# Two attention mixers on one core: the next pair's scores move ahead of the odd head's transposes, and four roundings spread over four heads

## What is computed

```python
def layer(x, ctx, ...):
    q, k, v, ga, uf, gf, zc, bc, cc, gc = split_cols(hx @ w_in, PROJ_SIZES)
    q, k = axial_rope(q), axial_rope(k)             # 8 query heads, 2 key heads, 64 wide
    a = window_attention(q, k, v, kc, vc, sink_b)   # softmax with a sink, blocks of 128 queries
    f = fourier_mix(uf, w_fourier)                  # fft2, real part, then a small product
    s = short_conv_mix(zc, bc, cc, conv_w, conv_b)  # three taps
    y = gated_merge(a, ga, f, gf, s, gc, w_out)     # concat(a*silu(ga), f*silu(gf), s*silu(gc)) @ w_out
    x_new = x + gate * rmsnorm(y, g_post)
    # layer 0 does the same for the context tokens (context_attention)

def sink_softmax(s, sink_b):
    m = max(max(s), sink_b)
    e = exp(s - m)
    return e / (sum(e) + exp(sink_b - m))
```

## Time and profile before

| | |
|---|---|
| time, median of 3 runs | 2353.62 us (2348.67 to 2356.35) |
| the profiled execution | 2354.48 us |
| its span | 2352.7 us |
| PE busy | 2259.4 us, 96% of the span |
| DVE / ACT / POOL busy | 1145.2 (49%) / 857.0 (36%) / 176.3 us (7%) |
| mean granted PE clock | 0.983 of full |
| DMA | 315.53 MB, mean 134 GB/s |

### The profile page before, as it was taken

The page is one execution under the profiler, slowest core; times in us unless marked ns, Lnnn a source line. Parts: engine busy times, 40 slices in busy tenths (PEclk is TensorE's granted clock), DMA queues, the critical chain, the costliest instruction groups (busy, mean ns, idle before and its releaser), DMA issues. The chain is left out here.

```text
span 2352.7 us, 47201 instructions
## 1 busy us (share of the span) xinstructions
PE 2259.4 (96%) x19336; PEld 2106.7 (90%) x19336; DVE 1145.2 (49%) x1926; ACT 857.0 (36%) x1392; POOL 176.3 (7%) x150
## 2 busy tenths in 40 slices
PE   6999999999999999988999999999999999998998
PEld 5986798789999999976999999999999998978998
DVE  5226365653433345456553333354343445477665
ACT  4125444732221233248432222243222234456544
POOL 0003112100000010501200000010000010001000
PEclk8999999999999999998999999999999999999999
DMA  9653554355665344520355665342233233224573
GB/s 307 184 159 121 152 145 106 117 153 152 182 200 164 104 138 118 145 81 28 100 161 165 187 186 153 114 127 81 82 107 99 85 95 99 77 77 125 170 208 114
DMA packets 515886, 315.53 MB, mean 134 GB/s; under 512 B 16035, under 2 KB 513274, under 8 KB 515622
## 3 DMA queue, kind: packets, MB, share of 16 engines
q1 hardware_dynamic: 515160, 313.45, 45.4%
q10 hardware_dynamic: 590, 0.16, 0.0%
HBM read 312.50 MB, written 1.06 MB: 133 GB/s over the span
## 5 line engine op out<-in xcount | busy, mean ns | idle before, releaser
L1051 PE MATMUL ps<-h_hi,w_hi 128*128 128x256 f32 x3424 | 745.5, 282 | 11.6 <-issue 3.6
L1051 PE MATMUL ps<-h_lo,w_hi 128*128 128x256 f32 x3424 | 734.4, 279 | 0.0
L1051 PE MATMUL ps<-h_hi,w_lo 128*128 128x256 f32 x3424 | 733.7, 279 | 0.0
L1051 PEld LDWEIGHTS ps<-h_hi,w_hi 128*128 128x128 f32 x3424 | 548.9, 189 | 39.8 <-issue 34.2
L1051 PEld LDWEIGHTS ps<-h_lo,w_hi 128*128 128x128 f32 x3424 | 549.7, 190 | 0.1
L1051 PEld LDWEIGHTS ps<-h_hi,w_lo 128*128 128x128 f32 x3424 | 549.5, 190 | 0.0
L1863 DVE TENSOR_TENSOR w_lo<-stage,w_hi 128x1024 fp32r<-128x1024 f32 x227 | 285.0, 1258 | 384.2 <-ACT w_hi L1386 383.8
L1386 ACT ACTIVATE w_hi<-stage 128x1024 fp32r<-128x1024 f32 x227 | 236.7, 1055 | 366.5 <-PE ps L1051 250.5
L1863 DVE TENSOR_TENSOR w_lo<-deep,w_hi 128x1024 fp32r<-128x1024 f32 x184 | 225.2, 1233 | 240.1 <-ACT w_hi L1386 238.4
L1386 ACT ACTIVATE w_hi<-deep 128x1024 fp32r<-128x1024 f32 x184 | 190.9, 1055 | 158.7 <-PE ps L1051 117.0
L1051 PE MATMUL ps<-g_hi,w_hi 128*128 128x256 f32 x1100 | 233.7, 281 | 0.6 <-DVE w_lo L1863 0.2
(11 more groups left out here) (406 smaller groups left out, 2825.6 us busy)
## 6 DMA issues: line engine op xcount, KB each, us to landing
modw<-in_ada_w SPq DMA_DIRECT2D x72, 1024.0 KB, 5.5
stage<-in_ffn_w_in SPq DMA_DIRECT2D x88, 512.0 KB, 5.0
deep<-in_ffn_w_in SPq DMA_DIRECT2D x88, 512.0 KB, 4.0
modw<-in_w_mod SPq DMA_DIRECT2D x18, 1024.0 KB, 7.6
stage<-in_w_in SPq DMA_DIRECT2D x30, 512.0 KB, 5.2
stage<-in_ffn_w_out SPq DMA_DIRECT2D x32, 384.0 KB, 3.3
stage<-in_even_w_in SPq DMA_DIRECT2D x24, 512.0 KB, 4.0
deep<-in_ffn_w_out SPq DMA_DIRECT2D x32, 384.0 KB, 3.4
```

The source lines that it names most:

```text
L1051: last = mm(ps[:, j, v - a:v - a + SEQ], w_part[wp][:, u % RING, c, :], x_part[xp][:, x, v:v + SEQ], start=first and wp == xp and v == a, ...
```

## The change

In `pe_mix1` the scores of pair m+2 are issued ahead of the transposes of odd head 2m+1, and no longer behind them. In `act_mix1` and `dve_mix1` the rounding of chunks 4 to 7, done in one go before, is done one chunk a head: on ACT behind E and K in the passes n = 11, 12, 13, 14, on DVE behind N(12), N(13), N(14), N(15). It concerns both mixers.

```diff
@@ pe_mix1
             for n in range(N):
-                transposes(n)
                 if n % 2 and n + 3 < N:
                     scores((n + 3) // 2)
+                transposes(n)
                 if n >= HEADS and n % HEADS == 3:
                     sums(n // HEADS - 1)
                 if n >= 2 and n % 2 == 0:
@@ act_mix1
                 if n == HEADS + 5:
                     act_feed(eng, p, (2,))
-                if n == HEADS + 3:
+                if HEADS + 3 <= n < HEADS + 7:
                     eng.wait_ge(S("conv_done"), p.at("conv_done", 1))
-                    for c in range(4, KC):
-                        act_high(p, c, mixT[:, c, 0:nt], nt)
+                    c = n - HEADS + 1
+                    act_high(p, c, mixT[:, c, 0:nt], nt)
@@ dve_mix1
                 if n == HEADS + 6:
                     dve_feed(eng, p, (2,))
-                if n == HEADS + 5:
-                    for c in range(4, KC):
-                        dve_low(eng, p, c - 4, c, nt)
+                if HEADS + 4 <= n < HEADS + 8:
+                    dve_low(eng, p, n - HEADS - 4, n - HEADS, nt)
                 if n >= HEADS and n % HEADS == 1:
                     sums(n // HEADS - 1)
                 if n >= HEADS and n % HEADS == 5:
                     gated(n // HEADS - 1)
```

## The result

The changed kernel takes 2361.02 us (median of 10 runs, 2353.64 to 2365.23), the kernel before beside it 2353.60 us (10 runs, 2347.72 to 2358.05): a ratio of 1.0029, with an interval of 1.0015 to 1.0042. It is slower, by 7.4 us in these runs, at the edge of the 0.3% that I called measurable.

A forecast was written before the change was run, and what follows sets the result against it. PE was taken to bound both head loops. Losses of 3.4 us in the first mixer and 2.0 in the second, 5.4 together, gave 2359.9 us profiled, 0.86 lower for the median: 2359.0 us, range 2353 to 2364.

The forecast's parts named there:

- V waits 0.23 where K isn't covered: Both mixers, eleven pairs: V idles 0.23 us each, waiting for copy K(odd), 2.5 us in all.
- Between pairs PE's sum is the same: PE, both mixers: the swap changes only distances between instructions; S of a pair stays 1.06 us, T 0.59.
- T(8) later by 1.24: Both mixers, transposes of head 8: start 1.24 us later through ACT's delayed queue, pairs 0 to 2 included.
- T(12)'s gap goes: First mixer, PE: spreading the roundings removes the 0.65 us gap at T(12), leaving it 0.8 us late.
- Chunk 5 holds G(0): First mixer, DVE: chunk 5's rounding waits for its ACT half behind K(11), holds G(0), makes N(14) 2.0 us late.
- Rival 2: The spread pays: chunk 5 does not hold G(0), T(12)'s 0.65 us is won; 2356.8 us, chance 0.15.
- V(7) +2.7: First mixer, values of pair 7: start 2.7 us later, mostly from N(15) coming 2.3 us late.
- First loop +3.4, second +2.0: Head loops of the two mixers: the first 3.4 us longer, the second 2.0, sum 5.4 us.
- Everything behind 440 us is the same, only shifted.: Profile behind both head loops: unchanged by the change, only later in time.
- 1 (copies hidden): Not slower: V finds K(odd) done, pair waits vanish and some gaps close; 2350.8 us, chance 0.08.
- 3 (all 24 pairs): Both mixers: every pair waits at V, 5.5 us for 2.5, total loss 8.4; 2362.0 us, chance 0.12.
- rival 4: End of second mixer: denser gaps lower the granted clock, 3 us lost; 2362.0 us, chance 0.05.

The follow-up runs named there:

- e5: Kernel before, PE's order kept but row sums one head earlier, weight splits and roundings moved to other heads; 2342.49 us, ratio 0.9965, in the later timing.
- e3: Kernel before with scores ahead of the odd transposes and V directly behind its pair's transposes, roundings in one go; profiled execution 2377.33 us.
- e1: Kernel before with only PE's swap, scores ahead of the odd transposes, roundings in one go; profiled execution 2354.73 us.
- e2: Kernel before with only the roundings spread one chunk a head, PE's order unchanged; profiled execution 2349.39 us.
- e4: Changed kernel with DVE's rounding of chunk 5 behind N(14), those of 6 and 7 behind N(15); profiled execution 2357.71 us.
- c2: Changed kernel with no edit, profiled a second time; execution 2353.89 us.
- f1: Changed kernel with no edit, third profile, from the later timing; median there 2353.92 us, ratio 1.0016 against the kernel before.
- c1: Kernel before with no edit, profiled a second time; execution 2349.03 us.

## Why the prediction was right, and where it was off

Forecast 2359.0 us, range 2353 to 2364, 0.75 on no measurable change, for +5.4 us in the loops. Measured: 2361.02, +5.16 in the loops. The sign, the place and the size of the loss in the loops were as worked out. That the median came out within about 2 us of the forecast is in part luck: it lost 7.4 us against the kernel beside it in the first timing and 3.7 in the second. Point by point:

1. **PE bounds the loops, and waits for ACT alone.** Every gap of the change is ended by ACT (at T(14) and S(9) ACT had itself waited for DVE, 0.38 us ahead of E(14) and 0.87 ahead of E(15)), and e5 shows that nothing but order made them: without work removed, 4.63 us of idle became 0.71.
2. **V waits 0.23 where K isn't covered.** By starts the seven pairs named for the first mixer cost 1.66 us, forecast 1.61, and beside pairs 7 and 15, which were worked out apart, no other pair waits. Two errors cancel in it. "Between pairs PE's sum is the same" does not hold: T(odd) and the next T in one piece take 0.16 us less than the 2 x 0.59 of the sum. By as much the cover is shorter, so the rows show more idle than forecast (0.25 to 0.32 a pair, 2.08 in all) for the same delay. e3 showed the dose. The Trainium skill (Perfetto Trace Analysis, Optimizing Tensor Performance) holds that rotating independent groups through PSUM banks lets evacuation overlap with the next matmuls. The banks do rotate here, the overlap is real, and it was too short: 1.02 us of transposes from T(odd)'s start (0.59 and 0.43), against the 1.34 to 1.41 until K(odd) let V start. By the rule alone these waits would be nothing, and the rows say otherwise.
3. **T(8) later by 1.24.** From the loop's start it came 1.16 later, in the second mixer 1.13. The term that was oversized is the 0.88 from E(7) to K(6): here it is 0.76. ACT in the change, K(5), E(7), K(6), E(8), counterpart of the earlier trace rows:

```profile
214.99 0.60 ACT L2221 ACTIVATE vtok<-ps 128x512 f32<-128x512 f32 x1 [1.07 <-PE ps L2130]
215.48 0.68 ACT L2205 ACTIVATE vtok<-ps,small 128x512 f32<-128x512 f32 x1
...
216.24 0.59 ACT L2221 ACTIVATE hT<-ps 128x512 f32<-128x512 f32 x1
...
218.61 0.69 ACT L2205 ACTIVATE vtok<-ps,small 128x512 f32<-128x512 f32 x1
```

4. **T(12)'s gap goes.** It went; T(12) is 0.68 us late, 0.8 was forecast. ACT alone gained from the spread, as e1 (0.72 kept) and e2 (gone) show.
5. **Chunk 5 holds G(0).** N(14) +1.98, forecast +2.0; e4 undid it alone and got 0.5 back. The Trainium skill (Perfetto Trace Analysis, Optimizing Scalar/DVE Operations) says that breaking up instructions may let work finish sooner where ScalarE or VectorE cause bubbles unsaturated. Rival 2 was built on that mechanism. As placed by the change it won nothing (e2: +0.09 us in the first loop, +0.35 in the second counted from V(0)); placed elsewhere, with two other pieces moved too, it is part of the 6.5 us of e5. The rule is right on what may be won and silent on where the pieces go.
6. **V(7) +2.7.** +2.55; N(15) +2.11, where the working has 2.27. The 0.16 too much at N(15) is 0.06 at N(14) and 0.10 between N(14) and N(15), which took 2.65 us for the 2.75 of 0.99, 1.14 and 0.62; V(7) inherits it.
7. **First loop +3.4, second +2.0.** +3.24 and +1.92. What is missing in the first is what was too much at V(7). In the second the working took the roundings as half as long; four take 1.33 us for 2.18 on ACT and 1.42 for 2.50 on DVE, which hardly mattered: the extra wait at T(15) is 0.33, forecast 0.3. The lengths that I named for the second (34.9 to 36.9 us, from S(0)) were wrong, since the stretch at low clock at its start was shorter than in the profile of before (4.77 us from S(0) to T(0) for 6.02).
8. **"Everything behind 440 us is the same, only shifted."** The program is, its time isn't: 6.1 us more in this execution, 1.0 less in the next, both against the profile of before. The step that failed is the one from a single execution to the median, where I took a fixed 0.86 us between them; it scatters by several.

The rivals: 1 (copies hidden) fell with the V rows; 2 with e2; 3 (all 24 pairs) didn't come, in the change and in e1 only the pairs named wait, and pairs 7 and 15 as before or as worked out. A clock that falls within a loop (rival 4) is seen in e3 and e4, one execution each, but in no profile of the change.

What stays open: the first timing of the change gave +7.4 us and the second +3.7, around the loops' 5.2, with intervals that overlap. Whether the order in the loops has any effect on the rest isn't separated from scatter. Which of e5's three edits brings how much was not tried alone.

## What to carry to other kernels

On an in-order engine an instruction that waits costs what stands behind it, not itself: before moving one, list what is ready behind it, and what its input stands behind on the other engine. The work between a producer and its consumer on the bounding engine is cover; compare it with the whole round trip (1.02 us against 1.34 to 1.41 here, from the producer's start), not with the fact that there is some. Read delays from starts, since idle alone misses what the engine does faster in between. And measure a change of this size by the length of its own stage and by many runs, not by two spans, with the stage's first mark behind the place where the clock rises.

## What the hardware showed that I had not expected

Executions of one program, with first loops equal to 0.01 us, differ by 5.5 us (before: 2352.7 and 2347.2) and 9.4 us (the change: 2361.5 and 2352.1) in their span, through PE's busy time for the same matmuls, at mean granted clocks of 0.983 and 0.983, 0.981 and 0.982. The same idle, 2.82 to 2.84 us ahead of S(0) of the second mixer, was followed by S(0) rows of 1.13 us (c2, e1, e2 and f1 among others), 1.49 and 1.50 (the change, c1) and 2.08 (before): how long the low clock lasts behind one and the same gap differs from execution to execution, and with it the time from S(0) to T(0), 3.18 to 6.02 us. And the clock can fall late in a sparse loop: to 0.50 in e4 from 254 us on, behind waits of 1.40 and 0.53 us that left it at 1.00 in the profiles of before and of the change. It cost 1.3 us there. Whether the pattern of gaps or chance decided it isn't shown by one execution.
